# A stack of layers with sparse experts: the low part of half of each expert's gate-up weights moves from VectorE to GpSimd

## The reference, cut to what matters

```
h = silu(einsum('bsd,edf->bsef', x, w_gate)) * einsum('bsd,edf->bsef', x, w_up)
h = h * combine[..., None]
return einsum('bsef,efd->bsd', h, w_down)
```

## Time and profile before

| what | value |
|---|---|
| device time, median of 3 | 1969.32 us (1968.93 to 1972.29) |
| the profiled execution: its own time | 1972.31 us |
| the profiled execution: span from first to last instruction | 1970.6 us |
| PE busy over the span | 1690.3 us (86%) |
| DVE, ACT, POOL busy | 1132.3, 901.4, 642.1 us |

### The profile page before, as it was taken

One profiled execution on the slowest core, in us unless ns is written; L12 is line 12 of the kernel. 1 busy time (PEld: TensorE's weight loads), 2 busy tenths in 40 slices (PEclk: granted clock), 3 DMA queues, 4 the chain that ended last, 5 costly groups with the idle time before them and its releaser, 6 DMA issues. The chain is left out here.

```text
span 1970.6 us, 21722 instructions
## 1 busy us (share of the span) xinstructions
PE 1690.3 (86%) x7906; PEld 1313.2 (67%) x7906; DVE 1132.3 (57%) x1591; ACT 901.4 (46%) x1371; POOL 642.1 (33%) x337
## 2 busy tenths in 40 slices
PE   5999997949982999987949991799896689999998
PEld 4876743738762876752738771687786578888887
DVE  3936566459865745656858985397454424233242
ACT  3246576248865235656328882435352331111112
POOL 2326631112211334731202210243622124444442
PEclk9999998969995999999969996899898899999999
DMA  4201021069954211020258972320000232223221
GB/s 187 86 33 45 20 67 59 6 279 374 379 204 196 88 52 45 1 71 16 86 214 336 377 299 119 133 107 22 21 1 1 85 128 97 105 87 107 86 85 43
DMA packets 40478, 233.91 MB, mean 119 GB/s; under 512 B 9316, under 2 KB 9700, under 8 KB 20660
## 3 DMA queue, kind: packets, MB, share of 16 engines
q1 hardware_dynamic: 31012, 215.46, 28.8%
q0 software_dynamic: 9216, 16.80, 2.3%
q10 hardware_dynamic: 144, 0.26, 0.1%
HBM read 226.03 MB, written 23.23 MB: 126 GB/s over the span
## 5 line engine op out<-in xcount | busy, mean ns | idle before, releaser
L259 PE MATMUL bank<-XS,WS 128*128 128x512 f32 x864 | 207.5, 403 | 15.7 <-DVE WS L384 15.7
L2537 POOL TENSOR_TENSOR WS<-ring,WS 128x2048 fp32r<-128x2048 f32 x31 | 149.3, 4817 | 188.2 <-ACT WS L2519 188.2
L259 PEld LDWEIGHTS bank<-XS,WS 128*128 128x128 f32 x864 | 166.0, 192 | 57.0 <-DVE WS L384 16.4
L1387 PE MATMUL bank<-WS,XS 128*128 128x512 f32 x768 | 188.5, 402 | 1.1 <-DVE XS L1498 1.1
L2519 ACT CAST WS<-ring 128x2048 fp32r<-128x2048 f32 x31 | 59.3, 1913 | 271.4 <-PE bank L2554 143.8
L2554 PE MATMUL bank<-XS,WS 128*128 128x512 f32 x768 | 174.8, 389 | 2.7 <-DVEq L2592 2.7
L2572 PE MATMUL bank<-WS,US 128*128 128x512 f32 x768 | 174.7, 389 | 0.0
L1387 PEld LDWEIGHTS bank<-WS,XS 128*128 128x128 f32 x768 | 145.9, 193 | 31.8 <-DVE XS L1498 1.9
L2554 PEld LDWEIGHTS bank<-XS,WS 128*128 128x128 f32 x768 | 144.1, 188 | 32.8 <-POOLq L2533 2.9
L2572 PEld LDWEIGHTS bank<-WS,US 128*128 128x128 f32 x768 | 144.1, 188 | 29.9
L1822 PE MATMUL bank<-XS,WS 128*128 128x512 f32 x576 | 135.6, 396 | 3.8 <-POOLq L2011 2.8
(11 more groups left out here) (531 smaller groups left out, 3422.6 us busy)
## 6 DMA issues: line engine op xcount, KB each, us to landing
raw<-in_w_exp SPq DMA_DIRECT2D x16, 2048.0 KB, 14.9
DN<-in_w_exp SPq DMA_DIRECT2D x32, 1024.0 KB, 11.4
ring<-in_w_ff SPq DMA_DIRECT2D x32, 1024.0 KB, 4.8
raw<-in_w_in SPq DMA_DIRECT2D x20, 1024.0 KB, 4.9
GU<-in_w_exp SPq DMA_DIRECT2D x8, 2048.0 KB, 17.4
XT<-in_w_exp SPq DMA_DIRECT2D x8, 2048.0 KB, 18.0
ring<-in_w_in SPq DMA_DIRECT2D x12, 1024.0 KB, 4.8
raw<-in_w_out SPq DMA_DIRECT2D x8, 1024.0 KB, 4.8
```

The costliest lines, as they stand in the source:

```text
L259: last = pe.matmul(m.ps[g % 8][:, :], WS[:, i % 2, hw, at:at + P], XS[:, hx, k, :], start=(step == 0), stop=(step == 3 * KD - 1))
L1387: last = pe.matmul(m.ps[2 + e % 2][:, :], r.XS[:, e % 2, hx, 4 * half + k, :], r.WS[:, half, hw, k * S:(k + 1) * S], start=(half == 0 and ...
L2537: pool.tensor_tensor(f.WS[:, q % 2, 1, :], f.ring[:, q % 4, :], f.WS[:, q % 2, 0, :].bitcast(F32), ALU.subtract).then_inc(w_low, 1)
```

## The change

For half 0, the low part of each expert's gate-up weights is formed by GpSimd; for half 1 still by VectorE. A new semaphore `up_low` counts GpSimd's subtractions, and TensorE and SyncE wait for it where they waited for VectorE's. GpSimd's program becomes, for each e: `low(e+1)`, `scatter(e-1)`, `gather(e+3)`.

```
             def gate_up_in(e):
                 if e >= 4:
-                    sp.wait_ge(w_low, 2 * (e - 3))
+                    sp.wait_ge(up_low, e - 3)
+                    sp.wait_ge(w_low, e - 3)
...
+            def low(e):
+                pool.wait_ge(w_high, 2 * e + 1)
+                pool.tensor_tensor(r.WS[:, 0, 1, :], r.GU[e % 4][:, 0:4 * S], r.WS[:, 0, 0, :].bitcast(F32), ALU.subtract).then_inc(up_low, 1)
+
             gather(0)
             gather(1)
+            low(0)
             gather(2)
             for e in range(NE):
-                if e == 0:
-                    gather(3)
-                if e + 4 < NE:
-                    gather(e + 4)
-                scatter(e)
+                if e + 1 < NE:
+                    low(e + 1)
+                if e:
+                    scatter(e - 1)
+                if e + 3 < NE:
+                    gather(e + 3)
+            scatter(NE - 1)
...
-                    pe.wait_ge(w_low, 2 * e + half + 1)
+                    pe.wait_ge((up_low, w_low)[half], e + 1)
...
-            def low(e, half):
-                dve.wait_ge(w_high, 2 * e + half + 1)
-                dve.tensor_tensor(r.WS[:, half, 1, :], r.GU[e % 4][:, half * 4 * S:(half + 1) * 4 * S], r.WS[:, half, 0, :].bitcast(F32), ALU.subtract).then_inc(w_low, 1)
+            def low(e):
+                dve.wait_ge(w_high, 2 * e + 2)
+                dve.tensor_tensor(r.WS[:, 1, 1, :], r.GU[e % 4][:, 4 * S:8 * S], r.WS[:, 1, 0, :].bitcast(F32), ALU.subtract).then_inc(w_low, 1)
...
-            low(0, 0)
-            low(0, 1)
+            low(0)
             rows_low(0)
             for e in range(NE):
-                if e + 1 < NE:
-                    low(e + 1, 0)
                 dve.wait_ge(silu_done, e + 1)
...
                 if e + 1 < NE:
-                    low(e + 1, 1)
+                    low(e + 1)
```

More of the change, by code:

```diff
@@ L1309, in experts @@
     names = ("hot_row", "table_done", "indexed", "dve_step", "xe_in0", "xe_in1", "ye_out0", "ye_out1", "gu_in0", "gu_in1", "gu_in2", "gu_in3", "dn_in0", "dn_in1", "row_t", "xe_high", "xe_low",
-             "w_high", "w_low", "gate_up", "silu_done", "hidden", "ht_done", "ht_high", "ht_low", "down_high", "down_low", "down", "ye_low", "ye_up")
+             "w_high", "w_low", "gate_up", "silu_done", "hidden", "ht_done", "ht_high", "ht_low", "down_high", "down_low", "down", "ye_low", "ye_up", "up_low")
     with stage(nc, "experts", *names) as (block, sems):
         hot_row, table_done, indexed, dve_step, xe_in0, xe_in1, ye_out0, ye_out1, gu_in0, gu_in1, gu_in2, gu_in3, dn_in0, dn_in1, row_t, xe_high, xe_low, \
-            w_high, w_low, gate_up, silu_done, hidden, ht_done, ht_high, ht_low, down_high, down_low, down, ye_low, ye_up = sems
+            w_high, w_low, gate_up, silu_done, hidden, ht_done, ht_high, ht_low, down_high, down_low, down, ye_low, ye_up, up_low = sems
         xe_in, ye_out = (xe_in0, xe_in1), (ye_out0, ye_out1)
```

## The result

The changed kernel takes 2024.6 us in the median of 4 executions (2020.05 to 2028.71); the kernel before took 1969.51 on the same chip. The ratio is 1.0281, with a 95% interval of 1.0263 to 1.03. That is 6.6 us above the upper end of the predicted range. The profiled execution took 2020.05 us with a span of 2018.3, 47.7 more than the span of before.

A forecast was written before the change was run, and what follows sets the result against it. It took TensorE as the bound, busy all the time, with transfer engines 99% occupied. Rounds of 10.34 us add 10.8 and 7.9 us, the head 3.0: about 21.5 on 1969.3 gives 1990.8 us, range 1979 to 2018.

The forecast's parts named there:

- The subtraction and the loop: Half 0's low part on GpSimd: 4.62 us against VectorE's 2.29, giving a buffer loop of 9.71 us without exclusion.
- the loop of the exclusion: Expert rounds: GpSimd and VectorE instructions each reading two SBUF tiles exclude each other, making 10.34 us a round; chance 0.62.
- the sum: Whole kernel: rounds add 10.8 us in the first layer and 7.9 in the second, head 3.0; together about 21.5.
- the race against part_low: Rival in expert rounds: GpSimd's subtraction starts before part_low's second instruction, giving 11.45 us a round, 2022 in all; chance 0.08.
- The head: Start of each layer's expert stage: later starts of 1.9, 0.4, 0.2 and 0.5 us, 3.0 together, some hidden.
- The gathers: Gathers issued one round closer to rows_t: landings of 5.9 and 7.7 us fit the about 7.8 free, costing nothing.
- P: The end of GpSimd's subtraction in an expert's round, from which the prediction timed the rest; next end at P + 10.34.
- Gathers late: Rival in expert rounds: transfers stay crowded, landings reach 9 to 10 us, rounds 11.04 to 11.54, 2010 to 2024; chance 0.20.

The follow-up runs named there:

- lead: The changed kernel, but behind scatter(e-1) GpSimd issues gather(e+4) again, as before the change, not gather(e+3); 1995.63 us, 1.0131 of the kernel before.
- bank: The changed kernel with VectorE's two-SBUF subtractions replaced by products with a zeroed bank, gathers still late; 2023.68 us, 1.0258 of the kernel before.
- late_gathers: The kernel before, all subtractions on VectorE, but with the change's order scatter(e-1), gather(e+3); 2020.44 us, ratio 1.0223.
- light: The changed kernel, transferring only half of each expert's down weights in the second layer from expert 2 on; 2012.06 us, 1.0206 of the kernel before.
- quarter: The changed kernel with gather(e+4) restored and GpSimd subtracting only 1024 of half 0's 2048 columns, VectorE the rest; 1974.89 us, 1.0023 of the kernel before.

## Why the prediction was wrong

**The subtraction and the loop: right.** The plain length is 4.60 to 4.62 (predicted 4.62), the loop of the exclusion 10.40 a round (10.34). Over 28 rounds that is 291.2 - 270.95 = 20.3 us, where the sum had 18.7. With the gathers in time (lead), the whole kernel takes 1995.63, inside the 1987 to 1998 that the prediction gave to this loop. GpSimd never won the race against part_low: no part_low instruction of the changed kernel took more than 1.23 us. The Trainium skill (SBUF — State Buffer, Who interferes with whom) has the exclusion that lead and bank now show from both sides: a VectorE subtraction of 4.4 us in lead, and in bank products with a bank operand, beside which GpSimd's subtraction keeps its 4.60.

**The head: too much.** gate_up_of(0) starts at 426.56 instead of 424.83 in the first layer, 1.7 us later (1.9 predicted). But the spans differ by only 0.5 more than the 28 rounds do, so of the head's 3.0 no more than that shows in the time.

**The gathers: the step that failed.** It is "Rounds of 10.3 leave them gaps, and the nearest rows are gathers from where the queue behind the weights was short: 5.9 and 7.7. Both fit." The rounds are 10.4, and the gaps aren't there: the transfer engines stay 93% occupied, and with lead, whose rounds are all 10.40, the landings in the first layer from 450 us on are 8.9 to 13.7. The two rows came from near the head of the stage. In the kernel before, the transfer engines were only 69% and 80% occupied in the 8 us ahead of those two gathers (issued at 448.6 and 1054.2), and the very next gathers took 13.2 and 13.6 us to land:

```profile
core 0: us, PE busy (x) PEld busy (x) DVE busy (x) ACT busy (x) POOL busy (x), PEclk, DMA share, GB/s
440.00:448.00 8.00, 8.00 (x42) 6.70 (x41) 8.00 (x9) 7.17 (x10) 1.38 (x1) 1.00 0.69 240
...
1046.00:1054.00 8.00, 8.00 (x42) 6.72 (x42) 6.96 (x6) 7.19 (x10) 1.22 (x1) 1.00 0.80 305
```

The step reasoned from occupancy without working it out: 99% of 9.3 us is 9.2 us of transfers a round, which by itself is 89% of 10.34, so little was freed.

**A term that was missed in the same step.** The gather was put at P + 2.39. In lead it is at P + 3.33, since the scatter ahead of it needs 2.88 us to issue, not 1.23: it ends 0.89 behind VectorE's subtraction (522.58 against 521.69 above). So gate_up_of starts on time, at P + 10.53, only if the gather lands within 10.53 - 3.33 - 1.07 (rows_t) = 6.1 us. GpSimd's wait for part_low absorbs 0.55 more, its 5.15 in lead less the plain 4.60, which makes 6.7 where the prediction had 7.8. Both limits are below the landings at the long stalls, 9.4 to 11.0 in the first layer, so by this working the term made the stalls longer, but without it they would have come too; bank, where the scatter takes 1.01, has them as well.

**What the stalls cost.** The 28 rounds take 318.1 us, 26.9 more than at 10.40. In the first layer it is 15.1 us, of which three rounds (14.40, 15.70, 14.77) hold 13.7; in the second 11.9, nearly all in the rounds of 14.86, 13.05 and 14.21 and the one behind the last of these (11.59). A stall is the late landing and a slower rows_t: 528.30 + 11.0 + 2.04 = 541.34, where gate_up_of starts (541.36); on time it would have been 525.66 + 10.40 = 536.06. So the rival "Gathers late" (11.04 to 11.54 a round, 2010 to 2024, a chance of 0.20) is what happened: transfers that stay crowded, late landings, a mean round of 11.36. Its form was another, though: it spread the loss over all rounds, and the trace has 24.6 of the 26.9 us in six of the 28, so that the mean fell between its bounds is in part luck. The 47.7 us of the profiled execution, set on the median of before as the prediction did, give 2017; the median of 2024.6 lies at the rival's upper end, while the stated range had stopped at 2018.

**What is left open.** The median lies 4.5 us above the profiled execution, and late_gathers varied by 28 us; I take it that the number of stalls varies, but only one execution of each is profiled: the shortest of four for the changed kernel and for lead, the longest for late_gathers, so that their mean rounds compare only roughly. What divides the transfer engines between the gathers and the weights, and so makes a landing 4 or 13 us, no run here shows; light shows only that fewer bytes of weights shorten it.

## What to carry to other kernels

When an instruction is put into an engine's queue, look at the transfers that the engine issues behind it, and price their landing at the occupancy that the new rounds will have, not by rows from where the queue was short. A landing hidden by one round of lead can be worth more than the instruction that was moved (50 us against 25 here), and costs behind the same wait don't add: removing one of them alone (bank) may show nothing. Where VectorE and GpSimd both read two SBUF tiles, a split of the work between them was a sequence here (quarter).

## What was not expected of the hardware

An indirect transfer's issue on GpSimd is held up by VectorE's two-SBUF instruction: 2.87 us in the median of the changed kernel's scatters, against 1.01 where VectorE reads a bank (bank). All but the last two scatters of each layer have such a subtraction beside them, and they end 0.87 to 0.91 behind it. The rows of before had it already: the scatter whose 1.23 us the prediction took as its length ended at 484.98, and the subtraction of VectorE beside it at 484.09, again 0.89 apart. So the 1.23 is no plain length: it holds the rest of a wait that had nearly run out when the scatter began.
